# Expert down matrices loaded by four neighbouring rows per partition, and gate and up sums turned with every fourth column

## Chip, cores and metric

The kernel runs on one NeuronCore of a Trainium2 chip. The metric is device time in microseconds of one execution. The weights lie in HBM; the core has 16 DMA engines, a TensorE (PE, its weight loads shown as PEld), a VectorE (DVE), a ScalarE (ACT), a GpSimd (POOL) and a SyncE (SP), which here only issues transfers.

## What is computed

Two transformer-like blocks over 512 tokens of width 1024, in float32. The change touches only the mixture of experts of the first block: 32 experts, two per token, each with a gate and an up matrix (1024 x 512) and a down matrix (512 x 1024).

```python
def hier_moe(h, w_router_group, w_router_expert, w_e_gate, w_e_up, w_e_down):
    ...
    x_rows = hf[row_tok].reshape(n_blocks, MOE_BLOCK, D)

    def expert_block(args):
        xb, e = args
        a = xb @ w_e_gate[e]
        u = xb @ w_e_up[e]
        return (jax.nn.silu(a) * u) @ w_e_down[e]

    y_rows = lax.map(expert_block, (x_rows, block_e)).reshape(n_rows, D)
    y = jax.ops.segment_sum(y_rows * row_w[:, None], row_tok, num_segments=T)
```

In `silu(a) * u` the 512 features of the expert stand in one order; the down product sums over them. Any order gives the same sum, if the rows of the down matrix are taken in the same one.

## The kernel before

Each expert gets a block of 64 token slots (`CAP`). A matrix comes from HBM in full float32. Because the products are done in a faster format with fewer bits, each matrix is split on the chip: ACT writes a rounded high part (`gate_hi`, `up_hi`, `down_hi`, line 884), and DVE the low part, which is the raw matrix less the high part (`low_half`, line 2351). The raw matrices have two buffers each, `ring_gate`, `ring_up` and `ring_down` (in the trace `gate`, `up`, `down`), for even and odd experts, and the low part is written over the raw one. The 64 rows of x also have a high and a low part, side by side as 128 columns of `xs`, so that one product with `gate_hi` and one with `gate_lo` give all four terms, as 128 rows of 512 features in a PSUM bank. The last eighth of gate and up goes through PE in plain float32 (line 1687).

ACT copies that bank to `g_sb` (for up, `u_sb`): 128 rows, the first 64 from the high part of x, the last 64 from the low part. `sum_of` (line 1712) adds the two halves and turns the result in one product: 128 columns of `g_sb` are the weights that PE loads, `twice` is two identities on top of each other, and the result has 128 features on the partitions and 64 slots beside each other. An expert has 8 such sums, four of gate and four of up. Then ACT takes the silu (`sg`), DVE multiplies (`gated`, tile `hx`), ACT and DVE write high and low parts (`hxs`), and `down_both` (line 1757) multiplies `hxs[:, f, :]` with `w[:, f, ...]` for f from 0 to 3. So the feature on partition p of block f must be the row of the down matrix that lies on partition p as its f-th.

The order is written out by hand, as a loop over pairs of experts. On PE a period is `gate_among` of expert e (the gate product, with the sums of expert e-1 and, every second time, the turning of the next pair's token rows, `turn_pair`, line 1659, among its steps), `up_both` of e, `down_both` of e-1. On DVE it is `gated` and `hx_low` of e-1, the gate's low part of e+1 around `x_low`, the up's low part of e+1, `y_sum` of e-1 (line 2386) and the down's low part of e. ACT follows the same order.

Transfers of the matrices are issued by SP, three per expert of 2 MB each, on one hardware queue: `next_gate`, `next_up` and `next_down` (lines 664, 668 and 672) wait until PE is done with the buffer, and then issue. Gate and up are laid out so that each partition gets eight neighbouring rows of 2 KB, 16 KB in one piece. Down before the change gets rows p, p+128, p+256 and p+384, four pieces of 4 KB. The token rows of a pair are gathered, and each expert's result rows are scattered to HBM (`put`, `scatter`, lines 815 and 796), by indirect transfers that POOL issues on another queue:

```python
            def put(e, p):
                pool.wait_ge(y_made, each(e, 1, 1))
                ...
                pool.wait_ge(scattered, each(e, 16, 32))
                ...
                nc.gpsimd.tensor_copy(put_row[p][:, :], table[:, bass.ds(each(e, 1), 1), 1]).then_inc(sem("put_ready"), 1)
                ...
                scatter(p)
```

The last wait means that the copy for expert e starts only after the scatter of expert e-1 has landed. `up_product` (line 1671) belongs to a path for experts with more than 64 tokens, which uses the raw matrices.

Of the kernel before, what the change touches and what calls it, by code (L numbers as in the profile page):

```python
# [24 lines left out]
P = 128  # L25
# [11 lines left out]
FC = FE // P  # L37
CAP = 64
# [190 lines left out]
def build_kernel(nc, t):  # L229

    with ExitStack() as ctx:
# [8 lines left out]
        def sem(name):  # L240
            if name not in sems:
# [5 lines left out]
        bank = [turned[:, 512 * (i // 3):512 * (i // 3) + 512] if i in (0, 3)  # L247
                else ctx.enter_context(nc.psum_tensor(f"bank{i}", [P, 512], F32)) for i in range(8)]
# [6 lines left out]
        def misc(name, shape, dt):  # L255
            size = int(np.prod(shape[1:])) * (2 if dt == BF16 else 4)
            x = at(name, shape, dt, place[0])
            place[0] += -(-size // 32) * 32
            return x
# [28 lines left out]
        twice = misc("twice", [P, CAP], F32)  # L288
# [3 lines left out]
        def temp(name, i, shape=(P, 512), dt=F32, extra=0):  # L292
            return at(name, list(shape), dt, T0 + i * 2048 + extra)
# [50 lines left out]
        g_sb, u_sb = temp("g_sb", 4), temp("u_sb", 5)  # L344
# [130 lines left out]
        for _, here, _, _, _, _ in head_steps():  # L475
            for key, _ in here:
                if slice_of(key) not in order_of_heads:
                    order_of_heads.append(slice_of(key))
# [39 lines left out]
        def ring_view(ring, n):  # L518
            _, parts, cols = slices[n]
            return ring[n % RINGS][:, 0:parts * cols].rearrange("p (c n) -> p c n", c=parts)  # L520
# [23 lines left out]
        def open_bank(pe, key):  # L544

            b, n = place_of[key]
            if n >= 1:
                pe.wait_ge(drained[b], n)
            return bank[b]
# [17 lines left out]

        plan = head_steps()
        in_pieces = {slice_no[key] for _, _, _, now, _, _ in plan for key, _ in now}

        def splits_before(n):
# [65 lines left out]
        def _(sp):  # L637
# [19 lines left out]

            gate_src = lambda e: t["w_e_gate"][bass.ds(e, 1)].rearrange("e (p c) n -> p (e c) n", p=P)
            up_src = lambda e: t["w_e_up"][bass.ds(e, 1)].rearrange("e (p c) n -> p (e c) n", p=P)
            down_src = lambda e: t["w_e_down"][bass.ds(e, 1)].rearrange("e (c p) n -> p (e c) n", p=P)  # L660

            def next_gate(e, p):
                sp.wait_ge(gate_done, each(e, 1, 1))
# [42 lines left out]
            with sp.Fori(0, NE // 2 - 2) as i:  # L706
                for k in range(2):
                    e, p = (i, 1 + k), (1 + k) % 2
# [15 lines left out]
            with sp.If(count > 0):  # L724
                with sp.Fori(0, OVF) as i:
                    with sp.If(count > i):
                        sp.wait_ge(sem("ovf_free"), i + 1)
                        e = expert_of(i)
# [690 lines left out]
        def _(pe):  # L1419
            def parts3(out, sh, sl, mh, ml, start, stop):  # L1420

                pe.matmul(out, sh, mh, start=start, stop=False)  # L1422
                pe.matmul(out, sh, ml, start=False, stop=False)  # L1423
                return pe.matmul(out, sl, mh, start=False, stop=stop)  # L1424
# [148 lines left out]
            for i, here, _, _, pt, o in plan:  # L1573
                if i is not None:
                    h, qt = i // TT, i % TT
                    j, x, n = h // 2, h % 2, (qt + 1) * P
# [4 lines left out]
                    out = open_bank(pe, ("S1", i))  # L1581
# [8 lines left out]
                if o is not None:  # L1590
# [3 lines left out]
                    out = open_bank(pe, ("O1", o))  # L1594
                    until_taken(pe, ("PT1", o))
                    for b in range(o % TT + 1):
                        ins = pe.matmul(out[:, 0:HD1], pT_t[o % 2][:, b, :], v1[:, b, (o // TT) * HD1:(o // TT + 1) * HD1],  # L1597
                                        start=b == 0, stop=b == o % TT)
# [39 lines left out]
            out = open_bank(pe, ("ranks", 0))  # L1638
# [4 lines left out]
            for b in range(TT):  # L1643
                ins = pe.matmul(out[:, TT * NE:(TT + 1) * NE], ones_b[:, :], hots[:, b, :, :].rearrange("p g e -> p (g e)"),
                                start=b == 0, stop=b == TT - 1)
# [3 lines left out]
            out = open_bank(pe, ("table", 0))  # L1649
            for q in range(TOPK * TT):  # L1650
                ins = pe.matmul(out[0:CAP, 0:NBLK], hot_slot[:, q, :], hot_block[:, q, :], start=q == 0, stop=q == TOPK * TT - 1)
# [5 lines left out]
            def turn_pair(c):  # L1657
                rows = xg[:, :].rearrange("t (p c) -> t c p", c=KC)
                return pe.transpose(turned[:, c * P:(c + 1) * P], rows[:, c, :], ident)
# [7 lines left out]
            def up_product(out, w, x, done):  # L1667

                for f in range(FC):
                    for c in range(KC):  # L1670
                        ins = pe.matmul(out[:, f * CAP:(f + 1) * CAP], w[:, c, f * P:(f + 1) * P], x[:, c, :],
                                        start=c == 0, stop=c == KC - 1)
                ins.then_inc(done, 1)

# [33 lines left out]
                pe.wait_ge(gated_made, each(e, 1))  # L1708

            def sum_of(k):  # L1710
                src, f = (g_sb, u_sb)[k // FC], k % FC
                return pe.matmul(bank[1][:, k * CAP:(k + 1) * CAP], src[:, f * P:(f + 1) * P], twice[:, :], start=True, stop=True)

            def sums(e):
                sum_waits(e)
                for k in range(2 * FC):
                    ins = sum_of(k)
                ins.then_inc(sums_done, 1)
# [52 lines left out]
            for c in range(KC):  # L1771
                ins = turn_pair(c)
# [12 lines left out]
            for f in range(FC):  # L1785
                if f % (FC // 2) == 0:
                    pe.wait_ge(down_lo_made, 2 * (NE - 1) + 1 + f // (FC // 2))
                for w in (down_hi_last, down_lo[1]):
                    for a in range(2):
                        ins = pe.matmul(bank[(3, 5)[a]][:, :], hxs_last[:, f, :], w[:, f, a * 512:(a + 1) * 512],  # L1790
                                        start=f == 0 and w is down_hi_last, stop=f == FC - 1 and w is not down_hi_last)
# [3 lines left out]
            with pe.If(count > 0):  # L1795
                with pe.Fori(0, OVF) as i:
                    with pe.If(count > i):
                        pe.wait_ge(sem("ovf_x"), i * 16 + 16)
                        pe.sem_inc(turn, 1)
                        turn_rows(sem("ovf_turned"))  # L1800
                        pe.wait_ge(sem("ovf_xt"), i + 1)
                        pe.wait_ge(sem("ovf_gate"), i * 16 + 16)
                        up_product(bank[2], ring_gate[0], xT, sem("ovf_gate_made"))
                        pe.wait_ge(sem("ovf_up"), i * 16 + 16)
                        up_product(bank[4], ring_up[0], xT, sem("ovf_up_made"))
                        pe.wait_ge(sem("ovf_hx"), i + 1)
                        pe.wait_ge(sem("ovf_down"), i * 16 + 16)
                        down_product(ring_down[0], hx, sem("ovf_y_made"))
# [10 lines left out]
            for h in range(MH):  # L1819
                for tp in range(2):  # L1820
                    out = open_bank(pe, ("v2", h, tp))
                    for a in range(2):
                        tk = slice((2 * tp + a) * P, (2 * tp + a + 1) * P)
                        for c in (2 * h, 2 * h + 1):
                            ins = parts3(out[:, a * MD:(a + 1) * MD], xmT_hi[:, c, tk], xmT_lo[:, c, tk], wh[:, c, :], wl[:, c, :],
                                         c == 2 * h, c == 2 * h + 1)
# [3 lines left out]
            for name in ("q2", "k2"):  # L1830
                wh, wl = weights(slice_no[(name, 0)])
                for j in range(KC):
                    h, a = j // 2, j % 2
                    out = open_bank(pe, (name, j))
                    for c in (2 * h, 2 * h + 1):
                        ins = parts3(out[:, :], wh[:, c, a * P:(a + 1) * P], wl[:, c, a * P:(a + 1) * P], xcT_hi[:, c, :],
                                     xcT_lo[:, c, :], c == 2 * h, c == 2 * h + 1)
# [3 lines left out]
            out = open_bank(pe, ("cols", 0))  # L1841
            for k, src in enumerate((g_i, g_e)):
                for tt in range(TT):
                    ins = pe.transpose(out[:, (k * TT + tt) * MH:(k * TT + tt + 1) * MH], src[:, tt * P:(tt + 1) * P],
                                       ident[0:MH, 0:MH])
# [5 lines left out]
            for h in range(MH + 1):  # L1851
                if h < MH:
                    out = open_bank(pe, ("mrow", h))
                    pick = pick_r[:, h:h + 1].to_broadcast([P, P])
                    pe.matmul(out[:, :], pick, neg_m[:, :], start=True, stop=True).then_inc(results, 1)
                    for sb in range(TT):
                        out = open_bank(pe, ("ST", h, sb))
                        n = (TT - sb) * P
                        for c in (2 * h, 2 * h + 1):
                            ins = pe.matmul(out[:, 0:n], k2T[:, c, sb * P:(sb + 1) * P], q2T[:, c, sb * P:SEQ],  # L1860
                                            start=c == 2 * h, stop=c == 2 * h + 1)
                        ins.then_inc(results, 1)
                if h >= 1:
                    g = h - 1
                    for tt in range(TT):
# [4 lines left out]
                        out = open_bank(pe, ("num", g, tt))  # L1870
                        for sb in range(tt + 1):
                            until_taken(pe, ("ST", g, sb))
                            w = sw[g % 2][:, starts[sb] + (tt - sb) * P:starts[sb] + (tt - sb + 1) * P]
                            ins = pe.matmul(out[:, 0:MD + 2], w, v2[:, sb, g, :], start=sb == 0, stop=sb == tt)
# [13 lines left out]
            for j in range(KC):  # L1888
                g, a = j // 2, j % 2
                out = open_bank(pe, ("pool", j))  # L1890
                for c in (2 * g, 2 * g + 1):
                    ins = parts3(out[:, :], wh[:, c, a * P:(a + 1) * P], wl[:, c, a * P:(a + 1) * P], poolT_hi[:, c, :],
                                 poolT_lo[:, c, :], c == 2 * g, c == 2 * g + 1)
# [21 lines left out]
            for tt in range(TT):  # L1915
                out = open_bank(pe, ("cin", 1, tt))
                tk = slice(tt * P, (tt + 1) * P)
                for c in range(KC):
                    ins = parts3(out[:, 0:192], hT_hi[2][:, c, tk], hT_lo[2][:, c, tk], wh[:, c, :], wl[:, c, :], c == 0, c == KC - 1)
# [23 lines left out]
            for s in range(4):  # L1943
                for name, c0, c1, n in (("uq", 0, nq, 2 * QKH), ("ukv", nq, 5, 512)):
                    wh, wl = weights(slice_no[(name, s)])
                    for tt in range(TT):
                        out = open_bank(pe, (name, s, tt))
                        tk = slice(tt * P, (tt + 1) * P)
                        for c in range(c0, c1):
                            ins = parts3(out[:, 0:n], cT_hi[:, c, tk], cT_lo[:, c, tk], wh[:, c - c0, :], wl[:, c - c0, :],  # L1950
                                         c == c0, c == c1 - 1)
# [860 lines left out]
```

## Time and profile before

| | |
|---|---|
| time, median of 3 runs | 1891.53 us (1890.48 to 1893.15) |
| profiled execution, its own time | 1886.33 us |
| span in that profile, first to last instruction | 1884.2 us |
| busy: PE, PEld, DVE, ACT, POOL | 92%, 75%, 61%, 52%, 12% |
| DMA packets, MB | 127043, 326.47 MB |
| each gate, up, down transfer | 2048 KB, 32 of each |
| their median time from issue to landing | 17.0, 17.3, 18.3 us |

Busy shares are means over stages with different limits; the experts' stretch lies between about 650 and 1160 us of the span. A matmul's duration in the trace overlaps the next one's, so busy PE is not PE at its peak. The time from issue to landing holds the time in the queue behind earlier transfers.

### The profile page before, as it was taken

To read this page: it belongs to the slowest core of one execution; us is meant where nothing else is said; L and a number is where in the kernel's file an instruction comes from. 1 tells how busy PE (TensorE), PEld (TensorE's weight loads), DVE (VectorE), ACT (ScalarE), POOL (GpSimd) and SP (SyncE) were. 2 spreads that over 40 slices of the span, in tenths; PEclk is the share of its full clock that TensorE was granted. 3 is DMA by queue.
4 is the path that set the end of the run, shared out by engine and by line. 5 is a ranking of instruction groups with operands and counts; after the bars stand their busy time and mean duration, and the time that the engine had idled before them with its cause. 6 is when DMAs were issued, how large, how long until landed. Compare 5 with 4: busy or idle time off the path is not lost.

```text
span 1884.2 us, 23249 instructions
## 1 busy us (share of the span) xinstructions
PE 1742.8 (92%) x8654; PEld 1419.8 (75%) x8654; DVE 1157.4 (61%) x1650; ACT 984.6 (52%) x1366; POOL 234.0 (12%) x174
## 2 busy tenths in 40 slices
PE   6999999999999599999999994899999999998999
PEld 5888878888788477777777773788788888887567
DVE  3543435444564599999999995771647643537452
ACT  4222234444432399999888984554353223557330
POOL 0000001010000124444232331010010000000000
PEclk9999999999999699999999997899999999999799
DMA  6755357434144699999999995232022332223001
GB/s 143 107 97 79 112 90 62 69 58 66 39 145 182 218 385 421 421 422 422 422 421 422 421 373 196 79 111 91 23 90 90 120 113 96 94 61 102 1 1 67
DMA packets 127043, 326.47 MB, mean 173 GB/s; under 512 B 8176, under 2 KB 80624, under 8 KB 118768
## 3 DMA queue, kind: packets, MB, share of 16 engines
q1 hardware_dynamic: 121360, 315.85, 51.1%
q0 software_dynamic: 5168, 8.92, 1.3%
q8 instruction: 56, 0.92, 0.2%
q10 hardware_dynamic: 432, 0.56, 0.1%
q14 instruction: 27, 0.22, 0.0%
HBM read 319.02 MB, written 15.21 MB: 177 GB/s over the span
## 4 chain that ended last, share of the span: by engine, by line
PE 67%; DVE 11%; DMA 9%; issue 8%; ACT 4%; POOL 0%; DVEq 0%; SPq 0%; POOLq 0%; ACTq 0%
PE bank L1422 14%; PE bank L1424 13%; PE bank L1423 13%; DMA down<-in_w_e_down 6%; PE turned L1422 3%; PE turned L1423 3%; PE turned L1424 3%; DVE down_lo L2351 2%; PE bank L1757 2%; DVE gate_lo L2351 2%; DVE up_lo L2351 2%; PE bank L1502 2%; PE bank L1597 2%; PE bank L1970 1%; DMA gate<-in_w_e_gate 1%
## 5 line engine op out<-in xcount | busy, mean ns | idle before, releaser
L2004 DVE TENSOR_TENSOR w_lo<-w_raw,w_hi 128x2048 fp32r<-128x2048 f32 (+2 forms) x76 | 163.8, 2157 | 286.9 <-ACT w_hi L884 286.8
L884 ACT ACTIVATE w_hi<-w_raw 128x2048 fp32r<-128x2048 f32 (+3 forms) x132 | 169.4, 1306 | 279.6 <-DMA w_raw<-in_w_in 75.6
L1422 PE MATMUL bank<-h1T_hi,w_hi 128*128 128x512 f32 x376 | 152.3, 405 | 0.0
L1424 PE MATMUL bank<-h1T_hi,w_lo 128*128 128x512 f32 x376 | 148.4, 395 | 0.0
L1423 PE MATMUL bank<-h1T_lo,w_hi 128*128 128x512 f32 x376 | 147.7, 393 | 0.0
L2351 DVE TENSOR_TENSOR down_lo<-down,down_hi 128x2048 fp32r<-128x2048 f32 x62 | 139.0, 2280 | 2.3 <-ACT down_hi L884 2.2
L2351 DVE TENSOR_TENSOR gate_lo<-gate,gate_hi 128x2048 fp32r<-128x2048 f32 x64 | 128.9, 2017 | 0.4 <-ACT gate_hi L884 0.3
L2351 DVE TENSOR_TENSOR up_lo<-up,up_hi 128x2048 fp32r<-128x2048 f32 x64 | 126.5, 2017 | 1.2 <-ACT up_hi L884 1.1
L884 ACT ACTIVATE down_hi<-down 128x2048 fp32r<-128x2048 f32 x62 | 115.1, 1905 | 16.2 <-DMA down<-in_w_e_down 16.2
L815 POOL COPY put_row<-table 64x1 int32 (+1 forms) x32 | 88.2, 2755 | 260.3 <-DVE ys L2386 258.1
L884 ACT ACTIVATE gate_hi<-gate 128x2048 fp32r<-128x2048 f32 x64 | 108.7, 1700 | 20.1 <-DMA h_dram<-h_tok 10.5
L1757 PE MATMUL bank<-down_hi,hxs 128*128 128x512 f32 x248 | 82.9, 416 | 32.6 <-DVE hxs L2380 32.6
L884 ACT ACTIVATE up_hi<-up 128x2048 fp32r<-128x2048 f32 x64 | 105.5, 1708 | 0.5 <-DMA up<-in_w_e_up 0.3
L1688 PE MATMUL bank<-gate_hi,xs 128*128 128x512 f32 x224 | 97.3, 434 | 3.4 <-DVE gate_lo L2351 1.8
L1757 PEld LDWEIGHTS bank<-down_hi,hxs 128*128 128x128 f32 x248 | 45.6, 194 | 65.3 <-DVE hxs L2380 34.4
L1688 PE MATMUL bank<-up_hi,xs 128*128 128x512 f32 x224 | 90.8, 405 | 0.0
L1689 PE MATMUL bank<-gate_lo,xs 128*128 128x512 f32 x224 | 89.2, 398 | 0.0
L1689 PE MATMUL bank<-up_lo,xs 128*128 128x512 f32 x224 | 87.7, 391 | 0.0
L1424 PEld LDWEIGHTS bank<-h1T_hi,w_lo 128*128 128x128 f32 x376 | 71.1, 189 | 15.6
L1422 PEld LDWEIGHTS bank<-h1T_hi,w_hi 128*128 128x128 f32 x376 | 71.9, 191 | 13.3
L1423 PEld LDWEIGHTS bank<-h1T_lo,w_hi 128*128 128x128 f32 x376 | 71.4, 190 | 13.4
L1757 PE MATMUL bank<-down_lo,hxs 128*128 128x512 f32 x248 | 78.9, 400 | 0.0
(673 smaller groups left out, 4462.8 us busy)
## 6 DMA issues: line engine op xcount, KB each, us to landing
gate<-in_w_e_gate SPq DMA_DIRECT2D x32, 2048.0 KB, 17.0
up<-in_w_e_up SPq DMA_DIRECT2D x32, 2048.0 KB, 17.3
down<-in_w_e_down SPq DMA_DIRECT2D x32, 2048.0 KB, 18.3
w_raw<-in_w_in SPq DMA_DIRECT2D x24, 1024.0 KB, 9.0
w_raw<-in_a_w_in SPq DMA_DIRECT2D x20, 1024.0 KB, 5.3
w_raw<-in_w_in SPq DMA_DIRECT2D x16, 512.0 KB, 9.0
w_raw<-in_a_w_out SPq DMA_DIRECT2D x8, 1024.0 KB, 5.0
w_raw<-in_c_w_in SPq DMA_DIRECT2D x6, 1024.0 KB, 5.1
```

The source lines that it names most:

```text
L815: nc.gpsimd.tensor_copy(put_row[p][:, :], table[:, bass.ds(each(e, 1), 1), 1]).then_inc(sem("put_ready"), 1)
L884: return nc.scalar.activation(out, in_, ACT.Copy, scale=scale)
L1422: pe.matmul(out, sh, mh, start=start, stop=False)
L1423: pe.matmul(out, sh, ml, start=False, stop=False)
L1424: return pe.matmul(out, sl, mh, start=False, stop=stop)
L1502: ins = pe.transpose(out[0:src.shape[-1], at_:at_ + n], src, ident)
L1597: ins = pe.matmul(out[:, 0:HD1], pT_t[o % 2][:, b, :], v1[:, b, (o // TT) * HD1:(o // TT + 1) * HD1], start=b == 0, stop=b == o % TT)
L1688: pe.matmul(out[:, :], x[:, c, :], wh[:, c, :], start=c == 0, stop=False)
L1689: return pe.matmul(out[:, :], x[:, c, :], wl[:, c, :], start=False, stop=c == KC - 1)
L1757: ins = pe.matmul(bank[6 + a][:, :], hxs[:, f, :], w[:, f, a * 512:(a + 1) * 512], start=f == 0 and w is down_hi, stop=f == FC - 1 and w i ...
L2004: V.tensor_tensor(ring_view(w_lo, n), ring_view(raw, n), ring_view(w_hi, n).bitcast(F32), ALU.subtract)\
L2351: V.tensor_tensor(lo[:, cs, :], raw_[:, cs, :], hi[:, cs, :].bitcast(F32), ALU.subtract).then_inc(lo_made_, 1)
```

## The change

The source of the down matrix is viewed so that partition p gets rows 4p to 4p+3, four neighbouring rows of 4 KB, 16 KB in one piece. To match, the sum f of gate and of up takes as weights the columns f, f+4, f+8, ... of `g_sb` and `u_sb` instead of 128 neighbouring ones, so that partition p holds feature 4p+f. The overflow path's `up_product` picks its weight columns in the same way. Numbers and sizes of all instructions and transfers on the engines stay.

```diff
-            down_src = lambda e: t["w_e_down"][bass.ds(e, 1)].rearrange("e (c p) n -> p (e c) n", p=P)
+            down_src = lambda e: t["w_e_down"][bass.ds(e, 1)].rearrange("e (p c) n -> p (e c) n", p=P)
...
-                        ins = pe.matmul(out[:, f * CAP:(f + 1) * CAP], w[:, c, f * P:(f + 1) * P], x[:, c, :],
+                        ins = pe.matmul(out[:, f * CAP:(f + 1) * CAP], w[:, c, :].rearrange("p (q f) -> p f q", f=FC)[:, f, :], x[:, c, :],
                                         start=c == 0, stop=c == KC - 1)
...
             def sum_of(k):
-                src, f = (g_sb, u_sb)[k // FC], k % FC
-                return pe.matmul(bank[1][:, k * CAP:(k + 1) * CAP], src[:, f * P:(f + 1) * P], twice[:, :], start=True, stop=True)
+                src, f = (g_sb, u_sb)[k // FC][:, :].rearrange("t (p c) -> t c p", c=FC), k % FC
+                return pe.matmul(bank[1][:, k * CAP:(k + 1) * CAP], src[:, f, :], twice[:, :], start=True, stop=True)
```

## Rows read from the trace of the kernel before

**Rows 1.** Page: busy shares, then GB/s in 40 slices.

```profile
PE 1742.8 (92%) x8654; PEld 1419.8 (75%) x8654; DVE 1157.4 (61%) x1650; ACT 984.6 (52%) x1366; POOL 234.0 (12%) x174
...
GB/s 143 107 97 79 112 90 62 69 58 66 39 145 182 218 385 421 421 422 422 422 421 422 421 373 196 79 111 91 23 90 90 120 113 96 94 61 102 1 1 67
```

**Rows 2.** Busy by stretch: PE, PEld, DVE, ACT, POOL, PEclk, DMA, GB/s.

```profile
681.00:865.00 184.00, 173.35 (x827) 135.21 (x826) 178.22 (x134) 169.05 (x165) 82.99 (x42) 1.00 1.02 422
881.00:1116.00 235.00, 215.69 (x1021) 168.16 (x1020) 221.13 (x165) 210.70 (x204) 78.91 (x54) 0.99 1.01 421
```

**Rows 3.** Timeline of DVE: four starts of y_sum (start us, us, what).

```profile
683.68 1.27 DVE L2386 TENSOR_TENSOR ys<-bank,y_low 64x512 f32<-64x512 f32 x2
...
880.89 0.68 DVE L2386 TENSOR_TENSOR ys<-bank,y_low 64x512 f32<-64x512 f32 x1
...
1038.60 0.68 DVE L2386 TENSOR_TENSOR ys<-bank,y_low 64x512 f32<-64x512 f32 x1
...
1116.38 0.68 DVE L2386 TENSOR_TENSOR ys<-bank,y_low 64x512 f32<-64x512 f32 x1
```

**Rows 4.** Tile in_w_e_down: 679 to 1097, then 690:750, then 870:930.

```profile
L672 SPq DMA_DIRECT2D down<-in_w_e_down x28: 383/384/389, 679.5 to 1096.6; - x28
...
DMA to landing us min/median/max: 10.7/18.5/19.6
...
DMA to landing us min/median/max: 11.5/12.0/12.6
...
DMA to landing us min/median/max: 19.0/19.3/19.6
```

**Rows 5.** Waits: 684 to 880, then 880 to 1100 (us in total, times, longest).

```profile
PE bank L1757 <- DVE hxs L2380: 11.9, 13, 1.4
...
ACT down_hi L884 <- DMA down<-in_w_e_down: 14.4, 14, 1.4
```

**Rows 6.** Timeline of SP, expert 0's issues; landings of gate, up, down.

```profile
583.19 0.43 SPq L654 DMA_DIRECT2D gate<-in_w_e_gate  x1
583.66 0.67 SPq L655 DMA_DIRECT2D up<-in_w_e_up  x1
584.37 0.52 SPq L656 DMA_DIRECT2D down<-in_w_e_down  x1
...
DMA to landing us min/median/max: 9.6/9.6/9.6
...
DMA to landing us min/median/max: 14.0/14.0/14.0
...
DMA to landing us min/median/max: 18.4/18.4/18.4
```

**Rows 7.** DMA in 593.5 to 597.0 (up), then 598.5 to 602.0 (down).

```profile
DMA packets 123, 1.47 MB, mean 421 GB/s; under 512 B 12, under 2 KB 12, under 8 KB 40
...
q1 hardware_dynamic: 123, 1.47, 99.2%
...
DMA packets 344, 1.36 MB, mean 390 GB/s; under 512 B 11, under 2 KB 11, under 8 KB 344
...
q1 hardware_dynamic: 344, 1.36, 97.4%
```

**Rows 8.** Weight loads: sums, then turn_pair, 700 to 860 (ns min/median/max).

```profile
L1712 PEld LDWEIGHTS bank<-twice,g_sb x80: 187/190/192, 710.4 to 848.9; 128*128 128x128 f32 x80
...
L1659 PEld LDWEIGHTS turned<-const,xg x42: 204/217/228, 700.8 to 852.6; 128*128 128x128 f32 x42
```

**Rows 9.** Chain that ended last, at the last expert's sums (start us, us).

```profile
1140.38 3.13 PE bank L1712 x16
```

**Rows 10.** POOL from 684 to 880: copy and scatter; landing of the scatters.

```profile
L815 POOL COPY put_row<-table 64x1 int32 x13 | 52.3, 4020 | 91.6 <-DVE ys L2386 91.6
L796 POOL DMA_INDIRECT y_dram<-ys,put_row x13 | 14.5, 1118 | 11.2 <-POOL put_row L815 11.2
...
DMA to landing us min/median/max: 7.8/8.1/8.5
```

## Prediction

> **What bounds the kernel now.** I read the busy shares and the slices of the page first [rows 1]. In slices 16 to 23 the 16 DMA engines move a flat 421 or 422 GB/s; nowhere else in the span does the rate stay up. This is the heart of the experts' stretch, and all the change lies in it. I then cut it in two with busy times by stretch [rows 2]. In both, the DMA share is 1.01 or 1.02, so the DMA engines have work all the time. DVE is busy 178.22 of 184 us in the first (97%) and 221.13 of 235 (94%) in the second. Two things are near their limit, and the question is which ends each expert's period.
>
> The starts of y_sum on DVE, one per expert, answer it [rows 3]. From 683.68 to 880.89 lie 13 periods, 197.21 us, 15.17 each. From 880.89 to 1116.38 lie 15 periods, 235.49 us, 15.70 each (28 periods in all, as many as down matrices are issued there [rows 4]). The first part is DVE's own pace; the second is 0.53 us an expert slower. Over 15.17 us a period the second part loses 235.49 - 15 x 15.17 = 7.94 us, of which 157.71 - 10 x 15.17 = 6.01 us by the tenth period (1038.60).
>
> The time from issue to landing of the down matrices says why [rows 4]. It is about 12 us at 690 to 750 and 19.3 at 870 to 930, where it stays (18.5 is the median over all 28 issued between 679.5 and 1096.6). The DMA queue is slower than DVE all along; the two buffers per matrix give it a lead, which is used up at about 880, and from there on the queue sets the pace. The waits agree [rows 5]: ACT's down_hi waits for the DMA of down 14 times after 880, 14.4 us in all, while before 880 PE waits for DVE's hxs, 11.9 us in 13 times. The DMA time of a matrix counts, then, from the first transfer of the unbroken queue, as lead first and as time later, until 7.94 us are regained; beyond that DVE's 15.17 us bound.
>
> **Part 1: down in 16 KB pieces.** Removed are 512 packets of 4 KB per matrix; added are 128 of 16 KB, as gate and up have them already. Two readings of the price:
> - Landings with nothing beside them, expert 0 [rows 6]: gate 583.19 + 9.6 = 592.8, up 583.66 + 14.0 = 597.7, down 584.37 + 18.4 = 602.8. Up took 4.9 us, down 5.1: **0.2 us** less if down becomes as up is.
> - Packet times in the same two transfers [rows 7]. In 3.5 us 16 engines have 56 us. In down's window 344 packets, 11 of them tiny, take 97.4%: 54.5 us, over the other 333 pieces 164 ns each. In up's window 99.2%, 55.6 us, hold 28 pieces of 4 KB (40 under 8 KB less 12 tiny), 4.6 us, and 83 of 16 KB: 51.0 us, 614 ns each. Four small ones take 655 ns, so a large one saves 41 ns; there are 128 on 16 engines, 8 on each: **0.33 us**.
> I take 0.27, the middle, and keep 0.20 and 0.33 for the range. It counts for the 28 matrices of [rows 4]; 23 of them are in by 1038.60. At 0.27 the queue gains 23 x 0.27 = 6.2 us by then, over the 6.01 lost, and 7.56 by 1116.38, where 7.94 were lost: 0.4 stays, gain **7.5 us**. At 0.20: 5.6 us. At 0.33: 9.2, capped at 7.94 by DVE.
>
> The Trainium skill (DMA: Bandwidth & Descriptors, "Why small descriptors are slow") gives a fixed overhead of about 3 cycles per packet inside the DMA engine, on 32 bytes a cycle. By it four pieces of 4 KB cost 524 cycles and one of 16 KB 515; at the 850 MHz of that page's bandwidth section that is 10.6 ns, an estimate of 0.085 us a matrix and 2.4 us in all. The rows show 41 ns where it gives 10.6; it stands behind the second rival.
>
> **Part 2: the sums with every fourth column.** Same count: 8 sums per expert, 16 passes of the array (the x16 of [rows 9]). Only the weight load of g_sb or u_sb changes, from neighbouring columns to every fourth, 16 bytes apart. No row shows that step. The nearest are the same load contiguous, median 190 ns, and turn_pair's load of xg with every eighth column, median 217, at most 228 [rows 8]. Bounds: 0 and 38 ns a pass, 0 and 0.6 us an expert; below nothing is excluded, since the contiguous load is the best case of the same data. I take turn_pair's median, 27 ns, 0.43 us an expert. In DVE's pace it lies behind PE's wait for hxs, 11.9/13 = 0.92 us an expert [rows 5]; in the queue's pace behind 0.53 us more. At the end there is no cover: the last expert's 16 passes stand on the chain [rows 9], so **+0.4 us** once (0 to 0.6). Were the cover gone everywhere, it would be 0.43 x 31 = 13 us.
> The Trainium skill (SBUF — State Buffer, the note on "cachelines") has lines of 16 bytes: each access that crosses to a new line pays, so four fp32 is where free strides end. Both steps, four and eight, would pay alike by it: 0.43 or 0.6 us an expert. By a price that shrinks with the stride it would be half. The sum moves by 0.2 us, but the rule speaks against counting this part at nothing.
>
> **Part 3: what comes with it.** The overflow path's up_product changes too and runs nowhere in this profile: nothing. Downs of experts 0 and 1, loaded before the unbroken queue, are in long before use: nothing. ACT, DVE and the down product work on the same shapes: nothing. The issue on SP has no work behind it that is late: the queue holds three or four transfers. The scatter of y is weighed as a rival.
>
> **Sum.** -7.5 + 0.4 = -7.1 us. The profiled execution's own time is 1886.33 (span 1884.2, 2.1 around it), so 1879.2. The timed runs have a median of 1891.53, 5.2 us above it; I take the same gain from that, rounded to 7: **1884.5 us**, -0.37%. If those 5.2 us are more time at the queue's pace, the cap of 7.94 is higher there and 9.2 is open.
>
> **Rivals.**
> - **DVE takes over wholly**, gain 8 to 9.2: the queue falls behind DVE for the whole stretch; for it, the 0.33 us of [rows 7]; against it, the cap in this trace. 1882.3 to 1883.5.
> - **The large piece is hardly faster** than four small ones. For it: the 0.2 us of the landings are read to 0.1 each, and down's window had other edges than up's (390 against 421 GB/s counts started and unfinished pieces). With a third of 0.2 to 0.27 us, 0.07 to 0.09 a matrix, 28 give 2 to 2.5 us; less 0.4, 1889.7, no difference that can be told. Against it: both readings are several times that. The skill's rule above lands here.
> - **Slower: the scatter of y closes POOL's ring.** An expert's put is a copy of 4.02 us, 0.86 us to the issue (11.2/13) and 8.1 us to landing, 13.0 of 15.17 us, and the next copy waits for that landing [rows 10]. The scatter shares the DMA engines with the queue. Its 64 rows are at most 4 on each engine; if each now waits for a 16 KB piece (614 ns) where a 4 KB one (164) stood, that is 1.8 us more: 9.9. It decides from 10.3. Against it: scatters run beside gate's and up's large pieces for two thirds of the time already. Were 8.1 to become 12, a period would be 16.9: 1.7 us over 13 periods and 1.2 over 15, 40 us: 1931. The skill (same DMA page, "Queues, rings and completion order") has each DMA engine take turns between queues a packet at a time, which is this mechanism; no row here shows the turns themselves.
> - **Slower: the strided load halves the array's rate of weights.** If 190 ns became 380, 16 passes cost 3 us against 0.92 of cover: 2.1 an expert over 31, some 60 us. It decides from 58 ns a pass; the load with stride eight costs 27.
>
> **Chances.** Forecast (gain 4 to 8) 0.63; DVE takes over 0.07; hardly faster 0.22; the two slower ones 0.08 together. A change under 0.2% (3.8 us) can't be told from none in this kernel. Faster 0.70, same 0.22, slower 0.08. The range from 1881.5 (9.2 gained, and nearly 1 us of spread between medians, as the runs shown have) to 1889.7 (the second rival's value) leaves out the slower cases and half of the second rival, near 2 in 10. The likeliest case's own range is 1883.5 to 1886.5 (gains of 8, the cap, to 5, which is 5.6 less 0.6).
>
> **What the next profile would show.** Packets 127043 - 32 x 384 = 114755. The starts of y_sum 15.17 apart until well past 960; in place of 7.94 us over that pace by 1116, 0 to 2.3. Down's time to landing creeps to 19 us much later or never. The flat rate stays at 421 to 425 GB/s, over a shorter stretch. The sums' weight loads near 217 ns; PE's wait for hxs shorter by 0.4 us an expert. Scatters at 8 to 10 us. The prediction is wrong if 16 KB pieces of down take over 640 ns, if the periods grow before 880 (POOL or PE), or if the slow part stays at 15.6 though down is faster, which would mean that the pace after 880 is not the queue's.

## The result and the profile after

The changed kernel takes 1892.01 us (median of 20 runs) where the kernel before takes 1888.7 (20 runs). The ratio is 1.0013, 95% interval 1.0007 to 1.0019: slower, by one to four us. The forecast was 0.37% faster, counted from 1891.53 us, a median of three runs that lay 2.8 us above that of the twenty. Ratios leave out three disturbed executions (one of 2530 us in experiment 1, two of 4412 and 6584 us in experiment 4).

The page of the changed kernel, its packets and the chain that ended last by engine and by line:

```profile
PE 1785.3 (94%) x8654; PEld 1479.7 (78%) x8654; DVE 1156.3 (61%) x1650; ACT 980.4 (52%) x1366; POOL 266.8 (14%) x174
...
DMA packets 114755, 326.47 MB, mean 173 GB/s; under 512 B 8176, under 2 KB 80624, under 8 KB 102384
...
PE 90%; DVE 3%; issue 3%; ACT 2%; DMA 1%; POOL 0%; SPq 0%; POOLq 0%; DVEq 0%; ACTq 0%
PE bank L1422 14%; PE bank L1424 13%; PE bank L1423 13%; PE bank L1757 6%; PE bank L1688 6%; PE bank L1689 5%; PE bank L1712 5%; PE turned L1422 3%; PE turned L1424 3%; PE turned L1423 3%; PE bank L1687 3%; PE bank L1502 2%; PE bank L1597 2%; PE bank L1970 1%; PE bank L1969 1%
```

The packets are the 114755 that were forecast. PEld is 60 us busier than in [rows 1], with the same count. The chain lies 90% on PE, and the sums (line 1712) stand on it with 5% of the span.

Busy time by stretch, the changed kernel, to be read against [rows 2]:

```profile
684.00:884.00 200.00, 200.00 (x876) 166.62 (x875) 189.61 (x143) 177.76 (x175) 90.22 (x44) 1.00 1.01 421
884.00:1117.00 233.00, 233.00 (x1025) 194.28 (x1024) 220.41 (x166) 208.26 (x204) 107.53 (x54) 1.00 1.01 422
```

PE is busy for all of both stretches, DVE only 95%. And four starts of y_sum on DVE, the answer to [rows 3]:

```profile
686.72 0.67 DVE L2386 TENSOR_TENSOR ys<-bank,y_low 64x512 f32<-64x512 f32 x1
...
888.06 0.68 DVE L2386 TENSOR_TENSOR ys<-bank,y_low 64x512 f32<-64x512 f32 x1
...
1043.19 0.68 DVE L2386 TENSOR_TENSOR ys<-bank,y_low 64x512 f32<-64x512 f32 x1
...
1120.96 0.68 DVE L2386 TENSOR_TENSOR ys<-bank,y_low 64x512 f32<-64x512 f32 x1
```

Thirteen periods take 201.34 us, 15.49 each, where they took 15.17; the next fifteen take 232.90, 15.53 each, where they took 15.70. All 28 together: 434.24 against 432.70. The kernel lost 4.1 us where DVE had set the pace and regained 2.6 where the queue had. Growing periods before 880 are what the prediction named as a sign of being wrong.

Waits from 684 to 1100, and the time to landing of the up matrices in 870 to 930, the changed kernel; then the same landing in the kernel before:

```profile
ACT sg L1106 <- PE bank L1712: 44.9, 27, 2.1
```

```profile
DMA to landing us min/median/max: 11.7/12.3/12.3
```

```profile
DMA to landing us min/median/max: 17.4/18.9/19.7
```

ACT's silu now waits for the sums on PE in 27 periods; the kernel before has no such wait in this stretch. The wait for the DMA of down, 14.4 us in [rows 5], is gone, and the queue keeps its lead. The weight loads of the sums in the changed kernel, to be read against the first row of [rows 8]:

```profile
L1712 PEld LDWEIGHTS bank<-twice,g_sb x85: 307/329/334, 699.7 to 856.8; 128*128 128x128 f32 x85
```

329 ns where it was 190, and where I had put 217. On PE's own timeline a group of four passes, from its start to that of the next product, before and after:

```profile
743.66 0.55 PE L1712 MATMUL bank<-twice,u_sb 128*128 128x64 f32 x4
744.02 0.48 PE L1688 MATMUL bank<-gate_hi,xs 128*128 128x512 f32 x1
```

```profile
780.69 0.92 PE L1712 MATMUL bank<-twice,u_sb 128*128 128x64 f32 x4
781.42 0.48 PE L1688 MATMUL bank<-gate_hi,xs 128*128 128x512 f32 x1
```

0.36 us before, 0.73 after: 0.37 for four passes, and as much where turnings follow (0.38 before, 818.29 to 818.67, and 0.76 after, 792.30 to 793.06). That is some 91 ns a pass, 1.46 us an expert.

The cover, what PE can lose before it falls behind DVE, is more than the 0.92 us of its wait for hxs. It shows from the last two passes of the up product to the third pass of the down product, in two neighbouring periods before, then in one after:

```profile
809.77 1.02 PE L1687 MATMUL bank<-up,xs 128*128 128x512 f32 x2
...
812.58 0.62 PE L1757 MATMUL bank<-down_lo,hxs 128*128 128x512 f32 x2
...
825.70 1.02 PE L1687 MATMUL bank<-up,xs 128*128 128x512 f32 x2
...
827.82 0.63 PE L1757 MATMUL bank<-down_lo,hxs 128*128 128x512 f32 x2
```

```profile
786.85 1.02 PE L1687 MATMUL bank<-up,xs 128*128 128x512 f32 x2
...
788.18 0.62 PE L1757 MATMUL bank<-down_lo,hxs 128*128 128x512 f32 x2
```

2.81 and 2.12 us before, the shorter one in the periods with turnings; 1.33 after, in every period, where PE waits for nothing. So 1.48 and 0.79 us fell away, 1.14 on average: the 0.92 that are recorded as a wait, and 0.2 around it. 15.17 + 1.46 - 1.14 = 15.49 us, which is the period of the changed kernel (15.49 and 15.53).

### The profile page after: what moved, and what is told of

Read it like the earlier page. It is cut to its first block, busy times and chain, and to the rows that moved or that the text cites. A ratio compares the mean times of both kernels' runs of the same rounds, so it can differ in the third digit from the quotient of the medians.

```text
span 1890.5 us, 23249 instructions
## 1 busy us (share of the span) xinstructions
PE 1785.3 (94%) x8654; PEld 1479.7 (78%) x8654; DVE 1156.3 (61%) x1650; ACT 980.4 (52%) x1366; POOL 266.8 (14%) x174
## 2 busy tenths in 40 slices
DMA packets 114755, 326.47 MB, mean 173 GB/s; under 512 B 8176, under 2 KB 80624, under 8 KB 102384
## 4 chain that ended last, share of the span: by engine, by line
PE 90%; DVE 3%; issue 3%; ACT 2%; DMA 1%; POOL 0%; SPq 0%; POOLq 0%; DVEq 0%; ACTq 0%
PE bank L1422 14%; PE bank L1424 13%; PE bank L1423 13%; PE bank L1757 6%; PE bank L1688 6%; PE bank L1689 5%; PE bank L1712 5%; PE turned L1422 3%; PE turned L1424 3%; PE turned L1423 3%; PE bank L1687 3%; PE bank L1502 2%; PE bank L1597 2%; PE bank L1970 1%; PE bank L1969 1%
## 5 line engine op out<-in xcount | busy, mean ns | idle before, releaser
L815 POOL COPY put_row<-table 64x1 int32 (+1 forms) x32 | 122.4, 3825 | 229.4 <-DVE ys L2386 227.2
L1757 PE MATMUL bank<-down_hi,hxs 128*128 128x512 f32 x248 | 90.7, 448 | 0.0
L1422 PE MATMUL bank<-h2T_hi,w_hi 128*128 128x512 f32 x200 | 78.2, 391 | 0.2 <-issue 0.2
```

The source lines that it names most:

```text
L1757: ins = pe.matmul(bank[6 + a][:, :], hxs[:, f, :], w[:, f, a * 512:(a + 1) * 512], start=f == 0 and w is down_hi, stop=f == FC - 1 and w i ...
```

## Experiments

All ratios are to the kernel before.

**1. The pieces alone.** Only the source of down is changed:

```diff
-            down_src = lambda e: t["w_e_down"][bass.ds(e, 1)].rearrange("e (c p) n -> p (e c) n", p=P)
+            down_src = lambda e: t["w_e_down"][bass.ds(e, 1)].rearrange("e (p c) n -> p (e c) n", p=P)
```

> The down matrices in 16 KB pieces, the sums with neighbouring columns as before, so features and rows of the down matrix no longer match: the product is computed on mismatched rows. Theory A (the strided weight load made PE the bound of the changed kernel, and the pieces do what was forecast): weight loads back at 190 ns, y_sum periods 15.17 us almost throughout, 28 periods in 425 to 427 us where before they took 432.7; 5 to 8 us under before, ratio 0.9958 to 0.9974. Theory B (the large pieces themselves slow the core, by the ports of SBUF or by the other queue): the loads of weights stay above 250 ns or the periods stay at 15.5; ratio 1.000 to 1.002.

Measured: 1883.66 us, ratio 0.997 (0.9962 to 0.9979). Its stretch from 700 to 1100 by engine, then that of the kernel before:

```profile
700.00:1100.00 400.00, 374.89 (x1790) 292.41 (x1789) 385.52 (x289) 365.76 (x354) 173.65 (x91) 1.00 1.01 427
```

```profile
700.00:1100.00 400.00, 371.09 (x1758) 289.20 (x1757) 381.13 (x285) 360.93 (x350) 155.14 (x91) 1.00 1.02 422
```

The first and the last start of y_sum in its 28 periods:

```profile
688.75 0.68 DVE L2386 TENSOR_TENSOR ys<-bank,y_low 64x512 f32<-64x512 f32 x1
...
1116.27 0.67 DVE L2386 TENSOR_TENSOR ys<-bank,y_low 64x512 f32<-64x512 f32 x1
```

427.52 us, 5.2 fewer. The first 18 periods take 15.17 us, the other ten are mostly longer, up to 16.06, at the queue's pace; I had expected 15.17 in nearly all. The queue moves 427 GB/s in place of 422. Weight loads are at 190 ns. The pieces do make the kernel faster, and theory B falls.

**2. The stride alone.** The sums as changed, down in four pieces as before; against the kernel before:

```diff
-                src, f = (g_sb, u_sb)[k // FC], k % FC
-                return pe.matmul(bank[1][:, k * CAP:(k + 1) * CAP], src[:, f * P:(f + 1) * P], twice[:, :], start=True, stop=True)
+                src, f = (g_sb, u_sb)[k // FC][:, :].rearrange("t (p c) -> t c p", c=FC), k % FC
+                return pe.matmul(bank[1][:, k * CAP:(k + 1) * CAP], src[:, f, :], twice[:, :], start=True, stop=True)
```

> The down matrices in four pieces of 4 KB as before, the sums with every fourth column, so here too rows and features do not match. Theory A: the weight loads take 329 ns and PE's period is 15.52 us; the queue's own sum of 28 periods (432.7 us) is near PE's 28 x 15.52 = 434.6, so PE sets the end: as slow as the changed kernel or up to 2 us slower, ratio 1.0010 to 1.0030. Theory B: loads at 190 ns, periods and time as before, ratio 0.9995 to 1.0005.

Measured: 1890.18 us, ratio 1.0012 (1.0003 to 1.0021), as slow as the whole change. Between 700 and 1100 PE is busy all the time here too:

```profile
700.00:1100.00 400.00, 400.00 (x1755) 333.46 (x1754) 378.69 (x284) 357.11 (x349) 176.60 (x91) 1.00 1.01 421
```

The two parts of the change do not add up. The stride alone costs 0.12%, the pieces alone give 0.30%, and both together cost 0.13%: behind PE the pieces are worth nothing.

**3. Half of the sums strided.** The changed kernel, with up's four sums on neighbouring columns.

```diff
-                src, f = (g_sb, u_sb)[k // FC][:, :].rearrange("t (p c) -> t c p", c=FC), k % FC
+                src, f = (g_sb, u_sb)[k // FC][:, :].rearrange("t (p c) -> t c p" if k < FC else "t (c p) -> t c p", c=FC), k % FC
```

> The changed kernel, but only the four sums of gate take every fourth column; those of up take neighbours, so up's features don't match. Theory A (PE has some 0.9 us an expert to spare, and only what goes beyond it counts): 8 strided passes cost about 0.6 us an expert, under the mean cover; periods at DVE's 15.17 us or, in the period with the turning of rows, where the cover is about 0.5 us, up to 0.1 more; ratio 0.9965 to 0.998. Rival (the loads' cost adds to the path in proportion, half of it for half the passes): periods near 15.35, ratio 0.9985 to 1.000.

Measured: 1884.92 us, ratio 0.998 (0.9971 to 0.9988). The thirteen periods that DVE sets are back at 15.17 us (684.01 to 881.22):

```profile
684.01 0.68 DVE L2386 TENSOR_TENSOR ys<-bank,y_low 64x512 f32<-64x512 f32 x1
...
881.22 0.68 DVE L2386 TENSOR_TENSOR ys<-bank,y_low 64x512 f32<-64x512 f32 x1
```

Eight dear passes, 0.7 us, lie wholly behind the cover; sixteen don't. The stretch from up's last passes to the down product's third is 2.06 or 1.37 us long here, so 0.73 and 0.04 of the cover are left. The price has a threshold, as theory A says; an added cost in proportion would show 15.34 here.

**4. More cover.** The changed kernel, with the last eighth of the up product left out on PE (the edit stops `both_halves` for up one chunk of rows early).

```diff
-                return pe.matmul(out[:, :], x[:, c, :], wl[:, c, :], start=False, stop=c == KC - 1)
+                return pe.matmul(out[:, :], x[:, c, :], wl[:, c, :], start=False, stop=c == KC - 1 or (low_made is up_lo_made and c == SPLIT_KC - 1))
...
-                for c in range(KC):
+                for c in range(SPLIT_KC if low_made is up_lo_made else KC):
```

> The changed kernel with all eight sums strided, but the last eighth of the up product (two passes of PE in plain float32, 0.86 us on the chain, an expert) is left out, so up's values lack that part. Theory A (PE alone had become the bound; DVE's 15.17 us wait right below): the passes still take about 329 ns, but PE's period falls from 15.52 by 0.86 to 14.66, DVE sets the pace again at 15.17, and then the queue: the stretch is as in the kernel with the pieces alone; ratio 0.9960 to 0.9980. Rival (the strided loads disturb DVE or ACT at SBUF, or the slower pace comes from another wait): periods stay over 15.3, ratio above 0.999.

Measured: 1884.47 us, ratio 0.9976 (0.9965 to 0.9988). All passes are as dear as in the changed kernel (mean 319 ns in both), yet DVE's pace is back (684.23 to 881.45, 197.22 us in thirteen periods):

```profile
684.23 0.68 DVE L2386 TENSOR_TENSOR ys<-bank,y_low 64x512 f32<-64x512 f32 x1
...
881.45 0.68 DVE L2386 TENSOR_TENSOR ys<-bank,y_low 64x512 f32<-64x512 f32 x1
```

So the strided loads as such slow neither DVE nor ACT: with all of them in place, both keep DVE's pace. What they cost is time on PE.

**5. The price by the step.** The eight sums of an expert take columns 1 to 8 apart, each on a line of its own (one execution, 1887.45 us). The file has one branch for each step:

```diff
+                s = lambda n: gu_sb[:, 0:n * P].rearrange("t (p c) -> t c p", c=n)[:, 0, :]
+                if k == 0:
+                    return pe.matmul(d, s(1), twice[:, :], start=True, stop=True)
...
+                return pe.matmul(d, s(8), twice[:, :], start=True, stop=True)
```

> The pieces of 16 KB, and the eight sums of an expert take columns 1, 2, 3, 4, 5, 6, 7 and 8 apart, each on a line of its own; the sums are of wrong columns, so the output is not the reference's. If the price comes with the line of 16 bytes (the Trainium skill, SBUF - State Buffer, cachelines), it starts where no two columns share a line: about 190 to 200 ns for 1 and 2, a little more for 3, 329 for 4, and the same from 4 to 8. If it comes from the step hitting the same part of the memory again, even steps are worse than odd ones: 4 and 8 at 329 or more, 3, 5 and 7 near 200. If eight is cheap, as turn_pair's 217 ns at step eight has it, 4 alone is dear.

Weight loads by line, costliest first (busy us, mean ns of one). Steps 1 to 7 are lines 1715, 1717, 1719, 1721, 1723, 1725 and 1727, step 8 is line 1728:

```profile
L1727 PEld LDWEIGHTS bank<-twice,gu_sb 128*128 128x128 f32 x52 | 16.0, 307 | 9.4 <-issue 6.3
L1728 PEld LDWEIGHTS bank<-twice,gu_sb 128*128 128x128 f32 x52 | 14.9, 334 | 0.0
L1721 PEld LDWEIGHTS bank<-twice,gu_sb 128*128 128x128 f32 x53 | 14.7, 324 | 0.0
L1725 PEld LDWEIGHTS bank<-twice,gu_sb 128*128 128x128 f32 x52 | 14.1, 318 | 0.0
L1723 PEld LDWEIGHTS bank<-twice,gu_sb 128*128 128x128 f32 x52 | 13.8, 304 | 1.1
L1719 PEld LDWEIGHTS bank<-twice,gu_sb 128*128 128x128 f32 x54 | 13.1, 251 | 1.2
L1715 PEld LDWEIGHTS bank<-twice,gu_sb 128*128 128x128 f32 x52 | 9.8, 188 | 2.1
L1717 PEld LDWEIGHTS bank<-twice,gu_sb 128*128 128x128 f32 x53 | 8.4, 197 | 0.0
```

188, 197, 251, 324 ns for steps 1 to 4, and between 304 and 334 from there to 8. Each step has a fixed place among the passes, and in the changed kernel the one step 4 spans 307 to 334 ns, so this spread says nothing of odd and even steps. From start to start on PE the four passes of steps 1 and 2 take 0.37 us (745.43 to 745.80), those of 3 and 4 0.67, of 5 and 6 0.69, of 7 and 8 0.73. The price begins at 3 and is full at 4. The Trainium skill (SBUF — State Buffer, the note on "cachelines") has 16-byte lines, which are four fp32; this trace agrees for the loads of the sums: they are cheap while each column shares its line with a neighbour, and dear where none does.

**6. The same steps in turn_pair.** The eight turnings take columns 1 to 8 apart, steps 1 to 7 on the odd lines from 1661 to 1673, step 8 on line 1674 (one execution, 1880.82 us). One branch for each step again:

```diff
+                if c == 0:
+                    return pe.transpose(d, s(1), ident)
...
+                return pe.transpose(d, s(8), ident)
```

> The pieces of 16 KB and contiguous sums; turn_pair's eight turnings take columns 1 to 8 apart, each on its own line, so x is put together from wrong columns and the output is not the reference's. If turnings are loaded in another way than plain float32 products, and the step costs little in it, all lines stay within 190 to 230 ns, 4 included. If the step of 8 is the cheap one for both kinds, the line with 4 shows about 330 ns here too.

The lines of steps 1, 2, 4 and 6:

```profile
L1671 PEld LDWEIGHTS turned<-const,xg 128*128 128x128 f32 x14 | 3.3, 233 | 0.0
...
L1667 PEld LDWEIGHTS turned<-const,xg 128*128 128x128 f32 x13 | 2.8, 218 | 0.0
L1663 PEld LDWEIGHTS turned<-const,xg 128*128 128x128 f32 x13 | 2.6, 201 | 0.0
L1661 PEld LDWEIGHTS turned<-const,xg 128*128 128x128 f32 x13 | 2.6, 197 | 0.0
```

Here every step stays between 197 and 233 ns, 4 included (218). From start to start on PE, two turnings take 0.15 us at steps 1 and 2 and 0.18 to 0.21 at the others (757.64 to 762.95). A turning's weight load pays little for a step, the load of a plain float32 product pays much. This row, of the turnings in the changed kernel, with the same step 8 as in [rows 8] and right behind strided sums, says that a load's duration is not its price:

```profile
L1659 PEld LDWEIGHTS turned<-const,xg x46: 204/277/353, 699.7 to 859.0; 128*128 128x128 f32 x46
```

The median is 277 ns in place of 217, and still two of them take 0.18 us on PE's timeline (793.06 to 793.24), as before (818.67 to 818.85). The row that I had taken the price from was of the cheap kind.

**7. A layout between.** Two pieces of 8 KB per partition (rows 2p and 2p+1 of either half), and sums with every second column; the whole computation.

```diff
-            down_src = lambda e: t["w_e_down"][bass.ds(e, 1)].rearrange("e (c p) n -> p (e c) n", p=P)
+            down_src = lambda e: t["w_e_down"][bass.ds(e, 1)].rearrange("e (h p c) n -> p (e h) (c n)", h=2, p=P)
...
-                src, f = (g_sb, u_sb)[k // FC], k % FC
-                return pe.matmul(bank[1][:, k * CAP:(k + 1) * CAP], src[:, f * P:(f + 1) * P], twice[:, :], start=True, stop=True)
+                src, f = (g_sb, u_sb)[k // FC][:, :].rearrange("t (h p c) -> t (h) c p", h=2, c=2), k % FC
+                return pe.matmul(bank[1][:, k * CAP:(k + 1) * CAP], src[:, f // 2, f % 2, :], twice[:, :], start=True, stop=True)
```

> A layout between the two, the computation whole: partition p holds rows 2p and 2p+1 of either half of the down matrix, two pieces of 8 KB, and a sum takes every second column (8 bytes apart) of its half. Theory A with a price by the line of 16 bytes (the Trainium skill, SBUF - State Buffer, cachelines): two hits per line, loads near 190 ns, PE under 15.17; the pieces save two thirds to all of what 16 KB saves; ratio 0.9962 to 0.998. Theory A with a price that grows with every stride over one: loads of 220 to 260 ns, half of 76 ns a pass, 0.6 us an expert, still under PE's cover of 0.9; ratio 0.997 to 0.999. Theory B: the loads follow the pieces' size, not the stride, and rise above 220 ns here for the 8 KB; 1.000.

Measured: 1883.62 us, ratio 0.9981 (0.9972 to 0.999). The loads take 196 ns, the 28 periods 429.47 us (684.11 to 1113.58), 3.2 fewer than before, and the queue moves 425 GB/s between 700 and 1100: 60% of what 16 KB saves, and the sums cost PE almost nothing. The time of the whole kernel does not tell this layout from the pieces alone (0.9981 and 0.997, with overlapping intervals).

**8. The sorting on ACT, sorted reads.** The pieces of 16 KB; ACT's two copies per expert from PSUM read every fourth column and write neighbours, and the sums are those of before. The whole computation.

```diff
-                copy(g_sb[:, :], bank[2][:, :]).then_inc(gate_out, 1)
+                copy(g_sb[:, :].rearrange("t (c p) -> t c p", c=FC), bank[2][:, :].rearrange("t (p c) -> t c p", c=FC)).then_inc(gate_out, 1)
...
```

(The copy to `u_sb` is changed in the same way.)

> The pieces of 16 KB, and the sorting of the features moved to ACT: its two copies per expert from PSUM to g_sb and u_sb read every fourth column and write neighbours, so that PE loads neighbouring columns. The computation is whole. Theory A: loads at 190 ns; ACT has about 1.2 us an expert to spare (92% busy of 15.17), its copies take 0.58 us now. If they stay under 1.1 us each, the gain of the pieces alone is kept: ratio 0.9958 to 0.9974. If a copy grows to 2.3 us (four times), ACT's period is 17.4 us and the kernel some 60 us slower. Theory B: as the changed kernel, 1.000 to 1.002, with loads at 190.

Measured: 1881.36 us, ratio 0.9965 (0.9954 to 0.9977), the fastest kernel here that computes the whole. Its copies on ACT (700 to 1100; busy us, mean ns), which take what they took with neighbours:

```profile
L884 ACT ACTIVATE u_sb<-bank 128x512 f32<-128x512 f32 x26 | 15.5, 598 | 0.0
L884 ACT ACTIVATE g_sb<-bank 128x512 f32<-128x512 f32 x26 | 15.1, 581 | 0.0
```

28 periods take 427.36 us (685.78 to 1113.14), as with the pieces alone. This is 0.35% faster, near the 0.37% that I had forecast for the change, and not to be told from the pieces alone (0.30%, the intervals overlap).

**9. The sorting on ACT, sorted writes.** The same order reached the other way round: PSUM is read in order, and g_sb and u_sb are written with each next column 512 bytes on.

```diff
-                copy(g_sb[:, :].rearrange("t (c p) -> t c p", c=FC), bank[2][:, :].rearrange("t (p c) -> t c p", c=FC)).then_inc(gate_out, 1)
+                copy(g_sb[:, :].rearrange("t (c p) -> t p c", c=FC), bank[2][:, :].rearrange("t (p c) -> t p c", c=FC)).then_inc(gate_out, 1)
...
```

(Against experiment 8; the copy to `u_sb` likewise.)

> The sorting on ACT again, but its copies read PSUM in order and write g_sb and u_sb with every step 512 bytes on, four runs side by side; the computation is whole. Theory A: ratio 0.9955 to 0.9977 if the copies stay near 0.6 us, as with the sorted reads. Rival: the scattered writes cost ACT what scattered reads didn't; copies over 1.1 us make ACT the bound and the ratio rises above 0.998.

Measured: 1904.21 us, ratio 1.0074 (1.0061 to 1.0087).

```profile
L884 ACT ACTIVATE u_sb<-bank 128x512 f32<-128x512 f32 x25 | 27.8, 1110 | 0.0
L884 ACT ACTIVATE g_sb<-bank 128x512 f32<-128x512 f32 x25 | 26.7, 1069 | 0.0
```

The copies take 0.5 us more each, and the period grows to 15.86 us (689.75 to 1133.82, 28 of them): of 1.0 us added on ACT 0.69 come through. My limit of 1.1 us a copy was wrong. I had taken ACT's idle share, 8% of 15.17 us, for cover, but most of it is time in which ACT waits for others: here too, at 15.86 us, it waits for DVE's `hx` 26 times, 26.3 us in all. By the difference, what ACT could lose unnoticed was 0.3 us an expert.

## Why the prediction was wrong

- **What bounds the kernel before: right.** DVE's pace of 15.17 us, then the queue's: with the pieces alone the queue is quicker by 5.2 us over 28 matrices, and the first periods stay at 15.17.
- **Part 1, the term of the pieces: right mechanism, too large.** I took 0.27 us a matrix; the 28 periods say 5.2/28 = 0.19. That is the landings' 0.2, not the packets' 0.33. The packet times overcount. A likely reason, which no run tests, is that the small packets' times overlap on an engine: the DMA share was 1.02 before and is 1.01 with large pieces. The sum would have been 5.3 - 0.4, not 7.5 - 0.4. The second rival (hardly faster) falls with it: its 0.085 us a matrix is under half of what was measured.
- **Part 2, the term of the sums, is the step that failed.** "I take turn_pair's median, 27 ns, 0.43 us an expert", and the upper bound of 38 ns, both came from the weight load of a turning. The load of a plain product went up by 139 ns at half of the turning's step, and a pass on PE's timeline by 91: 1.46 us an expert, beyond the cover. The range should not have ended at 38 ns, since no row showed a strided load of this kind.
- **The cover** that this cost was held against was misread too, to the safe side: 0.92 us, the recorded wait, where 1.14 fell away on average, 0.79 and 1.48 by turns. At the forecast's 0.43 us, or its upper bound of 0.6, either would have been enough.
- **The rival that came true** is the fourth, and what it says did happen: a pass took 91 ns from start to start and takes 182, so the array gets its weights at half the rate. Its price was too high, 190 ns a pass, because it took the load's whole duration for time on PE; 91 came of it. PE's period is 15.5 us, 0.35 over DVE's, not 2.1. That there is a threshold, two experiments bear out: half the dear passes cost no period, and all of them with more cover cost none. Its value of 58 ns a pass they don't show; it lies between the 46 of experiment 3 (half of the passes at 91) and 91, and the average cover of 1.14 us puts it near 71. I gave the rival, with the scatter's ring, 0.08.
- **The Trainium skill's rule** (SBUF — State Buffer, the note on "cachelines") was read, but only half of it used: I wrote that by the 16-byte line both steps pay alike, which steps 4 to 8 confirm for the loads of the sums, and took the amount from the turnings, whose loads hardly pay at any step.
- **The scatter's ring** did not close: scatters landed in 7.7 us (median, 684 to 1100), no slower than the 8.1 of [rows 10].
- **The end.** The last expert's 16 passes take 3.96 us on the chain, 0.83 more than in [rows 9] (0.4 was forecast), and the last period grew by 1.23 us, 18.88 to 20.11. How much of that is the stride stays open, since TensorE's granted clock (the figure behind POOL's count) differs there. These are the 16 passes and then the down product before, the same two in the changed kernel, and the 16 passes with the pieces alone:

```profile
1140.38:1143.51 3.13, 3.13 (x17) 3.13 (x18) 3.13 (x2) 1.70 (x1) 0.00 (x0) 0.59 1.08 373
1143.51:1149.29 5.78, 5.78 (x17) 4.55 (x18) 1.65 (x3) 0.80 (x2) 0.00 (x0) 0.63 0.28 93
```

```profile
1145.11:1149.08 3.97, 3.97 (x17) 3.97 (x18) 3.97 (x2) 1.71 (x1) 0.00 (x0) 0.78 0.94 279
1149.08:1155.24 6.16, 6.16 (x17) 4.83 (x18) 0.91 (x3) 0.80 (x2) 0.00 (x0) 0.59 0.51 161
```

```profile
1140.27:1143.92 3.65, 3.65 (x17) 3.65 (x18) 3.65 (x2) 1.70 (x1) 0.00 (x0) 0.50 1.09 379
```

Passes with neighbouring columns took 3.13 us at 0.59 of the full clock and 3.65 at 0.50, the strided ones 3.97 at 0.78. The down product, whose loads did not change, takes 0.38 us more, at 0.59 in place of 0.63. The forecast left the clock out of this term.

- **The sum of the traces.** From the issue of expert 0's gate (583.19 before, 587.13 after) to the end of the span lie 1301.0 and 1303.4 us: 2.4 slower, with 1.5 in the 28 periods and 1.2 in the last; the rest, -0.3, lies before and behind them. The other 3.9 us of the two spans lie ahead of the experts, where the code is the same. 2.4 us are 0.13%, as is the measured ratio.

## What to carry over

A price needs a row of the same kind of instruction, in its mode and type as well as its pattern; where there is none, set the upper end by what would hurt and test that alone before trusting the sum. Take prices and cover from start to start on the timeline: neither a weight load's duration nor a recorded wait is the time gained or lost. When the engines and the queue of a loop lie close to each other (here PE at 14.0 us an expert without its waits, DVE at 15.2, the queue at 15.7), relief of one is worth only the distance to the next, and a change that relieves one and loads another can come out slower than before. Look for the place where a reordering is free: here in the copy that reads PSUM anyway, not in the weights of PE.

## What the runs showed of the hardware

- Weight loads of a plain float32 product, 128 columns, mean durations: 188 ns for neighbours, 197 at step 2, 251 at step 3, 304 to 334 from step 4 on; a pass from start to start is 91 ns at step 1 and 182 at step 4. Of a turning, behind loads of neighbouring columns: 197 to 233 ns at any step from 1 to 8. Why the two kinds differ stays open; a turning is also one pass where a sum is two.
- A turning's load shows 277 ns instead of 217 when strided loads stand before it, and takes no more time on PE (0.18 us for two).
- ACT reads every fourth float32 of PSUM as fast as neighbours (598 and 581 ns for 512 columns), but needs 1110 and 1069 ns when it writes SBUF with every next element 512 bytes on.
- Loads of 2 MB from HBM in pieces of 4, 8 and 16 KB on a third of the traffic: 422, 425 and 427 GB/s for the whole, between 700 and 1100 us.
- What an engine can lose unnoticed is not its idle time: 0.3 us of 1.2 on ACT, and on PE 1.14 where 0.92 are recorded as its wait.
